# Fourteen patterns of test matmuls ahead of the first real one, on one core

## The reference

```
h = rmsnorm(x, norm_g);  v, bg, cg, za, u, zb, ga, gb = split(h @ w_in)
ya = (bg * causal_conv3(cg * v, conv_w) * silu(za)) @ w_out_a
yb = gelu(s5_scan(u));   yb = yb * sigmoid(yb @ w_glu + b_glu)
yb = (yb * silu(zb)) @ w_out_b
x  = rmsnorm(x + (sigmoid(ga) * ya + sigmoid(gb) * yb) @ w_o, final_g)
# second layer: a gated spatial mix over 8 heads beside a forgetting attention over 16 heads
h = rms_norm(x, g2) * (1 + scale(c)) + shift(c);  z = h @ w_in_2
x = rms_norm(x + gate(c) * (concat(y_a, y_b) @ w_out_2), final_g_2)
```

## Time and profile before

| | us |
|---|---|
| median of 2 runs | 2668.69 (2667.31 to 2670.07) |
| the profiled execution, its own time | 2670.03 |
| its span in the trace | 2668.8 |
| PE busy | 2631.5 (99%) |
| DVE busy | 1638.4 (61%) |
| ACT busy | 845.1 (32%) |
| POOL busy | 390.9 (15%) |

### The profile page before, as it was taken

The page is one execution under the profiler, slowest core; times in us unless marked ns, Lnnn a source line. Parts: engine busy times, 40 slices in busy tenths (PEclk is TensorE's granted clock), DMA queues, the critical chain, the costliest instruction groups (busy, mean ns, idle before and its releaser), DMA issues.

```text
span 2668.8 us, 30016 instructions
## 1 busy us (share of the span) xinstructions
PE 2631.5 (99%) x11928; PEld 2159.8 (81%) x11928; DVE 1638.4 (61%) x2187; ACT 845.1 (32%) x1139; POOL 390.9 (15%) x295
## 2 busy tenths in 40 slices
PE   9989999999999999999999999999999999999997
PEld 7878888888888888888888888877888888888786
DVE  6678888787887765445444775556465563234434
ACT  5122222222222222222322332332565563233321
POOL 0034343433443421000000000010000000000001
PEclk9999999999999999999999999989999999999999
DMA  5233333333333333667555675623222222322333
GB/s 184 96 112 112 105 114 99 121 110 104 116 103 125 128 121 120 215 202 245 186 193 192 207 240 181 197 95 129 95 80 73 86 80 87 111 95 87 115 122 111
DMA packets 119867, 353.07 MB, mean 132 GB/s; under 512 B 15408, under 2 KB 22832, under 8 KB 119728
## 3 DMA queue, kind: packets, MB, share of 16 engines
q1 hardware_dynamic: 119728, 351.16, 39.7%
HBM read 321.68 MB, written 23.07 MB: 129 GB/s over the span
## 4 chain that ended last, share of the span: by engine, by line
PE 96%; DVE 2%; issue 1%; POOL 0%; ACT 0%; DMA 0%; SPq 0%; DVEq 0%; POOLq 0%; ACTq 0%
PE bank L512 29%; PE bank L513 28%; PE bank L514 28%; PE bank L678 2%; PE bank L680 2%; PE bank L679 2%; PE bank L721 1%; PE bank L711 1%; PE bank L576 1%; PE bank L564 1%; DVE X L1814 0%; PE bank L704 0%; PE bank L702 0%; PE bank L502 0%; DMA W<-in_w 0%
## 5 line engine op out<-in xcount | busy, mean ns | idle before, releaser
L1138 DVE TENSOR_TENSOR WL<-W,WH 128x1024 fp32r<-128x1024 f32 (+1 forms) x456 | 592.2, 1301 | 528.3 <-ACT WH L816 527.0
L816 ACT ACTIVATE WH<-W 128x1024 fp32r<-128x1024 f32 (+1 forms) x456 | 480.6, 1056 | 1008.6 <-PE bank L514 768.8
L512 PE MATMUL bank<-hH,WH 128*128 128x512 f32 x1792 | 700.3, 391 | 10.7 <-DVE WL L1138 6.8
L513 PE MATMUL bank<-hL,WH 128*128 128x512 f32 x1792 | 699.1, 390 | 0.0
L514 PE MATMUL bank<-hH,WL 128*128 128x512 f32 x1792 | 698.8, 390 | 0.0
L512 PEld LDWEIGHTS bank<-hH,WH 128*128 128x128 f32 x1792 | 337.1, 188 | 89.9 <-DVE WL L1138 7.2
L514 PEld LDWEIGHTS bank<-hH,WL 128*128 128x128 f32 x1792 | 337.1, 188 | 70.6
L513 PEld LDWEIGHTS bank<-hL,WH 128*128 128x128 f32 x1792 | 337.2, 188 | 70.2
L512 PE MATMUL bank<-h2H,WH 128*128 128x512 f32 x640 | 252.6, 395 | 0.1
L514 PE MATMUL bank<-h2H,WL 128*128 128x512 f32 x640 | 249.4, 390 | 0.0
L513 PE MATMUL bank<-h2L,WH 128*128 128x512 f32 x640 | 249.1, 389 | 0.0
(11 more groups left out here) (260 smaller groups left out, 3604.5 us busy)
## 6 DMA issues: line engine op xcount, KB each, us to landing
W<-in_w SPq DMA_DIRECT2D x335, 512.0 KB, 3.7
W<-in_ada SPq DMA_DIRECT2D x96, 512.0 KB, 4.4
W<-in_wa SPq DMA_DIRECT2D x32, 512.0 KB, 3.9
W<-in_wo SPq DMA_DIRECT2D x32, 512.0 KB, 3.9
W<-in_wvv SPq DMA_DIRECT2D x32, 512.0 KB, 3.7
W<-in_wb SPq DMA_DIRECT2D x16, 512.0 KB, 3.7
URAW<-U SPq DMA_DIRECT2D x96, 64.0 KB, 3.1
scr_am<-SO SPq DMA_DIRECT2D x16, 256.0 KB, 2.0
```

Of the source, the lines that this page charges most:

```text
L512: e.matmul(o, wh, xh, start=first, stop=False)
L513: e.matmul(o, wh, xl, start=False, stop=False)
L816: e.activation(WH[:, n % NB, c], W[:, i % NW, c], ACT.Copy).then_inc(sem["hi"], 1)
L1138: e.tensor_tensor(WL[:, s, c], W[:, plan.item_of[n] % NW, c], WH[:, s, c].bitcast(F32), ALU.subtract).then_inc(sem["lo_v"], 1)
```

## The change

Ninety-two fast 32-bit matmuls and twelve plain 32-bit ones with 32 rows stand ahead of the first real one, in place of eleven of the twelve identity matmuls; one identity matmul is left at the end and signals `test`. In order: 14 with 512 consecutive columns; six each of ten forms of 512 columns (consecutive; every second element; every fourth; two halves interleaved; sixteen parts interleaved; runs of 8 elements alternating; runs of 16 alternating; two rows of 256; consecutive, begun 8 elements later; one column repeated); six of 496 columns; six with 64 rows; six that accumulate into one result; and three rounds of four 32-row matmuls, each into a bank of its own. Their operands lie in the space of `U`. POOL fills them first, DVE makes one 32x32-block transpose of a test tile, and `keep_u` waits for the tests.

```diff
+        e.wait_ge(*nth("test", 2))
+        for _ in range(14):
+            e.matmul(bank[7][:, :], TW[:, :], TM[:, 0:512], start=True, stop=True)
+        two = TM[:, 0:512].rearrange("p (a b) -> p b a", a=2)
+        sixteen = TM[:, 0:512].rearrange("p (a b) -> p b a", a=16)
+        eights = TM[:, 0:512].rearrange("p (a b c) -> p b a c", a=2, c=8)
+        lines = TM[:, 0:512].rearrange("p (a b c) -> p b a c", a=2, c=16)
+        rows2 = TM[:, :].rearrange("p (a b) -> p a b", b=1024)[:, :, 0:256]
+        for m in (TM[:, 0:512], TM[:, 0:1024:2], TM[:, 0:2048:4], two, sixteen, eights, lines, rows2, TM[:, 8:520],
+                  TM[:, 0:1].to_broadcast([128, 512])):
+            for _ in range(6):
+                e.matmul(bank[7][:, :], TW[:, :], m, start=True, stop=True)
+        for _ in range(6):
+            e.matmul(bank[7][:, 0:496], TW[:, :], TM[:, 0:496], start=True, stop=True)
+        for _ in range(6):
+            e.matmul(bank[7][:, :], TW[0:64, :], TM[0:64, 0:512], start=True, stop=True)
+        for i in range(6):
+            e.matmul(bank[7][:, :], TW[:, :], TM[:, 0:512], start=i == 0, stop=i == 5)
+        for _ in range(3):
+            for i in range(4):
+                e.matmul(bank[4 + i][:, :], TQ[32 * i:32 * i + 32, 0:128], TQ[32 * i:32 * i + 32, :], start=True,
+                         stop=True)
+        e.matmul(bank[7][:, 0:128], IDT[:, :], IDT[:, :], start=True, stop=True).then_inc(sem["test"], 1)
...
+        e.memset(TM[:, :].bitcast(F32), 0.5)
+        e.memset(TW[:, :].bitcast(F32), 0.5).then_inc(sem["test"], 1)
+        e.memset(TQ[:, :], 0.5).then_inc(sem["test"], 1)
+        e.memset(TD[0][:, :], 0.5).then_inc(sem["test"], 1)
         e.memset(ONE[:, :], 1.0).then_inc(sem["const"], 1)
```

More of the change, by code:

```diff
@@ L44 @@
 SIGNALS = {
-    "par": 1, "const": 1, "w_first": 16, "hi_first": 1, "lo_first": 1, "hi": 1, "lo_v": 1, "used": 1,
+    "test": 1, "par": 1, "const": 1, "w_first": 16, "hi_first": 1, "lo_first": 1, "hi": 1, "lo_v": 1, "used": 1,
     "xh": 1, "xl": 1, "xsq": 1, "xacc": 1, "silu_c": 1,
@@ L203, in program @@
     YK = at("YK", 64, [128, 16, 512])
+    TM, TW = at("TM", 164, [128, 2048], F32R), at("TW", 172, [128, 128], F32R)
+    TQ = at("TQ", 173, [128, 512])
+    TD = [at(f"TD{i}", 176 + 2 * i, [128, 512]) for i in range(2)]
     W = at("W", 128, [128, NW, 1024])
@@ L606, in pe_program @@
         e.wait_ge(*nth("const", 4))
-        for _ in range(WARM):
-            e.matmul(bank[7][:, 0:128], IDT[:, :], IDT[:, :], start=True, stop=True)
+        e.wait_ge(*nth("test", 2))
[21 more added lines that the diff above has]
+        e.matmul(bank[7][:, 0:128], IDT[:, :], IDT[:, :], start=True, stop=True).then_inc(sem["test"], 1)
         for kc in range(2):
@@ L1398, in ssm_until @@
                 done[0] += 1
+        e.wait_ge(*nth("test", 2))
+        e.transpose(TD[1][:, :], TD[0][:, :])
         e.wait_ge(*nth("hi_first", 0))
@@ L1423, in keep_u @@
         def keep_u(m):
+            if m == 0:
+                e.wait_ge(*nth("test", 3))
             projected(u_p[m])
```

## The result

The changed kernel takes 2693.09 us (2692.36 to 2693.82, two runs) against 2668.69: a ratio of 1.0093, with a 95% interval of 1.0075 to 1.0111. The forecast was 2690.5, within 2683 to 2703. The span of the profiled execution went from 2668.8 to 2691.1, by 22.3 us, where 21.8 was forecast.

What follows compares the result with a forecast made beforehand. PE was taken as the bound, ending last for 96% of the span. Fills, tests, clock, patterns and row groups delay the first real matmul by 27.1 us, less 5.3 of holes: 2668.69 + 21.8 = 2690.5 us, range 2683 to 2703.

Steps and rivals of the forecast that it cites:

- PE bounds, so the block costs its own length: Start of PE's program: uncovered work lengthens the kernel by its own duration; first real matmul delayed 27.1 us.
- Fills: POOL at the start: four new fills delay PE's start by 2.8 us, from 1.96 to 4.8.
- Clock at the start: First tests: half rate for 5.1 us, 12 matmuls at 0.427 instead of 0.227, 2.4 us, bounds 1.6 to 2.8.
- Patterns: Tests whose moving operand has elements apart: 3.0 us extra for 30 matmuls, the middle of 0 and 6.0.
- five forms in doubt: Among the ten forms: every second, every fourth, two halves, sixteen parts, one column repeated; 30 matmuls of unknown price.
- the sum by the page (3.6): Patterns by the skill's 16-byte lines: every fourth and both interleaved forms slow, 18 x 0.200 = 3.6 us.
- The plain remainder: Tests priced as the stream: 0.2267 us a matmul, including 64 rows and accumulation; six of 496 columns, 1.3 us.
- Row groups: Twelve plain 32-bit matmuls of 32 rows in four row groups: side by side, 2.8 us; one after another, 11.1.
- The rival at 2699: The twelve plain 32-bit matmuls: row groups run one after another, +8.3 us, 2699 us; chance 13%.
- Holes: PE's start, first five units: 5.5 us of waits for input and slower steps, of which 5.3 are given back.
- The head start does not last: ACT's and DVE's lead is gone before the 6.75 us wait at 178 us; rival that it lasts: 2681, 4%.
- the one of plain 32-bit products: The 92 fast tests: rival that each runs as plain 32-bit at 0.93 us, giving 2752 us; chance 2%.

Runs made afterwards that it cites:

- the late block: The changed kernel with the tests moved behind the first four units of real matmuls and twelve identity matmuls back at the start: 2696.87 us, ratio 1.0108.
- the test of widths: The changed kernel with other tests: four widths, eight matmuls each, consecutive and in pairs 4 or 64 elements apart: 2681.13 us in one run.
- the test of forms: The changed kernel with another choice of tests, eight matmuls for each form, behind 20 consecutive ones: 2721.23 us in one run.

## Why the prediction was right

- **PE bounds, so the block costs its own length.** It held. The block was forecast to end at 34.2 and ended at 35.26; the whole was moved by as much, less the holes.
- **Fills.** PE starts at 4.77; forecast 4.8. What was not said: the fills' 2.8 us are paid only because the tests follow them. With real matmuls in that place, as in the late block, the holes swallow them.
- **Clock at the start.** Forecast 2.4 us; the first fourteen took 5.11 us in place of 14 x 0.227 = 3.2, so 1.9. Steps of half rate went on for some 4 us and not 5.1. Behind an idle stretch they lasted from 3.0 (the test of widths) to 6.1 us in these traces, so the size of this term is run-to-run chance. It is read from the steps alone: the view of stretches, of which the prediction says that it has no clock on record there, prints 1.00 for that time before the change as after it, while the test matmuls stepped at 0.427.
- **Patterns.** Forecast 3.0 as the middle of 0 and 6; measured 4.14 (17.74 - 13.60). The sum stayed under the bound of 6.0, but the price behind the bound did not hold: every second and every fourth element stepped at 0.456 on average, above the 0.43 that the prediction had named as a sign of being wrong, and eight parts reached 0.486 in the test of forms. The sum stayed low because two of the five forms in doubt cost nothing: steps of two and four, and sixteen parts, were slow; two halves and the repeated column were not. Runs of 8 and of 16, priced as the stream, stepped at 0.245. Which forms would be slow was not known, and that the middle of the range came within 1.1 us is luck. The Trainium skill (SBUF — State Buffer, "Door 1: The DMA port swizzle") would have two halves slow and every second element fast. The trace has it the other way round, 0.218 and 0.456, and that the sum by the page (3.6) came nearer is chance: the form that it has wrongly slow and the one that it has wrongly fast cancel.
- **The plain remainder.** The forms priced at the stream were too cheap by 0.6 us: 1.43 for six of 496 columns (forecast 1.3), 1.59 each for 64 rows and for accumulation (1.36). In the record of single starts the first two matmuls behind a change of row groups are 0.31 to 0.34 us apart.
- **Row groups** work side by side: 24 records in 32.23 to 35.02, 2.79 us, forecast 2.8. The rival at 2699 falls. The last identity matmul took 0.24 us, forecast 0.4.
- **Holes.** 5.3 forecast, 5.0 measured. The difference is a reading: the prediction took 39.81 for the start of the token sums, which is 39.34. From 7.07 that makes 32.27 us and, less 27.2, 5.1 of holes instead of 5.5. The late block, which meets no holes, gives back 0.1 us ahead of the wait for `WL`, so it is the holes and not the head start of ACT and DVE.
- **The head start does not last.** The wait for `WL` is 6.71 us, before 6.75. That rival falls too, as does the one of plain 32-bit products: consecutive tests step at 0.227.
- **Not foreseen:** 0.9 us less behind the holes, most of it from the clock's edges. Sum: 21.8 + 1.1 (block) + 0.3 (holes) - 0.9 = 22.3.

The mechanism was right: the block is on the path and costs its own length less the holes. That the spans met the forecast within 0.5 us is in part luck, since the block's terms were off by -0.5 (clock), +1.1 (patterns), +0.6 (remainder) and -0.2 (last matmul), and the clock took 0.8 back later.

The medians lie 24.4 apart and the profiled spans 22.3. Two runs of each kernel, up to 2.8 us apart among themselves, don't tell these two numbers apart. Fourteen further runs of the kernel before, beside the experiments, have medians of 2667.8 and 2667.7, which puts the two kernels some 25 us apart; the account above explains the 22.3 of the profiled pair, and not the rest.

## What to carry to other kernels

Work ahead of the first useful matmul of a kernel bound by TensorE costs its own length less the holes behind it; find the holes by counting steps from the first real matmul to a landmark, and price an unseen form from the stream's step to a little above the step at half clock: the slowest here took 0.486 us where half clock takes 0.427. And read what a test says of the kernel's own stream: here one unused test form stepped 5% faster than the form that the kernel uses some 11,000 times, which was worth 87 us once the operands were stored for it. A layout that makes one engine faster is paid by those that write it, so choose the order in which they write by their rows too.

## What the runs showed of the hardware

Fast 32-bit matmuls of 512 columns step at 0.227 to 0.229 us with consecutive columns, 0.216 with two places in turn, from 4 to 1024 elements apart, and 0.45 to 0.46 with every second or fourth element, at full clock. Eight parts in turn take 0.486. ACT and DVE write a row of 512 alternating between two places 1 KB apart in 1.1 to 1.2 us in place of 0.6 to 0.75 when they write singly, and up to 1.6 on average where such writes follow each other (`hH`, `hL`, `yH`); with every second element read and consecutive ones written the means are 0.80 to 0.90. Twelve plain 32-bit matmuls in four row groups take 2.79 us, 0.23 each; their records start in fours within 0.02 us. The first two steps behind a change of the number of rows are 0.31 to 0.34 us. Why consecutive columns are 5% slower than pairs is open.
